# Gated feed-forwards, down product: five of eleven units as seven block products, at positions 1, 3, 5, 6 and 8, with the first set of weight sums made in the up steps

## What is computed

```
def _swiglu_ffn(x, g_norm, w_gate_up, w_down):      # FFN_HIDDEN = 2816, D_MODEL = 1024
    h = _rms_norm(x, g_norm)
    gate, up = jnp.split(h @ w_gate_up, 2, axis=-1)
    return (jax.nn.silu(gate) * up) @ w_down
```

## Time and profile before

| | us |
|---|---|
| median of 3 runs (lowest, highest) | 1206.88 (1206.46, 1207.20) |
| the profiled execution, device time | 1207.01 |
| its span, first to last instruction | 1205.3 |
| PE busy | 1197.1 (99% of the span) |
| PE weight loads busy | 1028.9 (85%) |
| DVE busy | 945.8 (78%) |
| ACT busy | 705.1 (59%) |
| POOL busy | 54.8 (5%) |
| HBM read | 218.31 MB |

### The profile page before, as it was taken

One profiled execution on the slowest core, in us unless ns is written; L12 is line 12 of the kernel. 1 busy time (PEld: TensorE's weight loads), 2 busy tenths in 40 slices (PEclk: granted clock), 3 DMA queues, 4 the chain that ended last, 5 costly groups with the idle time before them and its releaser, 6 DMA issues.

```text
span 1205.3 us, 17062 instructions
## 1 busy us (share of the span) xinstructions
PE 1197.1 (99%) x6787; PEld 1028.9 (85%) x6787; DVE 945.8 (78%) x1133; ACT 705.1 (59%) x821; POOL 54.8 (5%) x105
## 2 busy tenths in 40 slices
PE   9999999999999999999999999999999999999998
PEld 7888888888899888888888888988888888988886
DVE  5566476669786686767978995999987998699986
ACT  7655264555465665555638565577654765477752
POOL 2000000000010000000010020000001011000000
PEclk9999999999999999999999999999999999999999
DMA  9644636555654335655554444455564434556550
GB/s 347 239 157 165 237 140 215 193 185 179 238 191 170 132 140 209 210 177 189 188 205 167 148 144 170 174 211 189 196 216 169 146 105 175 180 187 209 195 192 35
DMA packets 32567, 220.36 MB, mean 183 GB/s; under 512 B 3889, under 2 KB 4049, under 8 KB 6769
## 3 DMA queue, kind: packets, MB, share of 16 engines
q1 hardware_dynamic: 29888, 212.33, 49.6%
q0 software_dynamic: 1664, 5.41, 1.3%
q10 hardware_dynamic: 944, 1.64, 0.4%
HBM read 218.31 MB, written 1.05 MB: 182 GB/s over the span
## 4 chain that ended last, share of the span: by engine, by line
PE 92%; DVE 6%; DMA 1%; issue 0%; POOL 0%; ACT 0%; ACTq 0%; POOLq 0%; DVEq 0%
PE acc L1969 16%; PE acc L1971 16%; PE acc L1970 16%; PE tb L2003 10%; PE acc L2003 9%; PE tb L2006 5%; PE acc L2006 5%; PE tb L2013 3%; DVE cacc L1645 3%; DVE wlo L1212 1%; PE acc L2333 1%; PE acc L2335 1%; PE acc L2336 1%; PE tb L1970 1%; PE tb L1971 1%; PE tb L1969 1%
## 5 line engine op out<-in xcount | busy, mean ns | idle before, releaser
L1212 DVE TENSOR_TENSOR wlo<-raw,whi 128x2048 fp32r<-128x2048 f32 x184 | 418.9, 2287 | 124.4 <-ACT whi L625 124.4
L625 ACT ACTIVATE whi<-raw 128x2048 fp32r<-128x2048 f32 (+1 forms) x198 | 370.3, 1883 | 115.4 <-PE acc L1971 69.5
L1969 PE MATMUL acc<-whi,xth 128*128 128x512 f32 x448 | 179.5, 401 | 0.4 <-DVE xtl L1310 0.3
L1971 PE MATMUL acc<-whi,xtl 128*128 128x512 f32 x448 | 174.9, 390 | 0.0
L1970 PE MATMUL acc<-wlo,xth 128*128 128x512 f32 x448 | 174.5, 390 | 0.0
L1969 PE MATMUL acc<-whi,yth 128*128 128x512 f32 (+1 forms) x428 | 168.7, 394 | 0.0
L1971 PE MATMUL acc<-whi,ytl 128*128 128x512 f32 (+1 forms) x428 | 166.5, 389 | 0.0
L1970 PE MATMUL acc<-wlo,yth 128*128 128x512 f32 (+1 forms) x428 | 166.2, 388 | 0.0
L2003 PE MATMUL tb<-xhl,whi 128*128 128x512 f32 x512 | 121.9, 390 | 0.0
L2003 PE MATMUL acc<-xhl,whi 128*128 128x512 f32 x480 | 114.2, 390 | 0.0
L2003 PEld LDWEIGHTS tb<-xhl,whi 128*128 128x128 f32 x512 | 94.9, 188 | 19.4 <-issue 0.5
(11 more groups left out here) (422 smaller groups left out, 1752.2 us busy)
## 6 DMA issues: line engine op xcount, KB each, us to landing
raw<-in_stream SPq DMA_DIRECT2D x200, 1024.0 KB, 4.9
rb<-in_rel_rows POOLq DMA_DIRECT2D x8, 256.0 KB, 2.9
x<-in_x_in ACTq DMA_DIRECT2D x4, 256.0 KB, 7.3
raw<-in_stream SPq DMA_DIRECT2D x2, 512.0 KB, 9.2
gs_sb<-in_gs_row POOLq DMA_DIRECT2D x1, 1024.0 KB, 7.8
frow<-in_fin_row POOLq DMA_DIRECT2D x2, 512.0 KB, 4.7
raw<-in_stream SPq DMA_DIRECT2D x2, 256.0 KB, 6.9
ws_sb<-in_ws_t POOLq DMA_DIRECT2D x1, 512.0 KB, 7.5
```

The lines of the kernel that those rows point to most:

```text
L625: act.activation(whi[:, s, c0:UNIT], raw[:, s, c0:UNIT], ACT.Copy).then_inc(hi_ready, 1)
L1212: dve.tensor_tensor(wlo[:, s, :], raw[:, s, :], whi[:, s, :], ALU.subtract).then_inc(lo_ready, 1)
L1969: pe.matmul(o, xh, wh, start=first, stop=False)
L1971: return pe.matmul(o, xl, wh, start=False, stop=last)
```

## The change

`SEVEN` goes from 4 to 5 and `SEVEN_POS` from (2, 4, 6, 7) to (1, 3, 5, 6, 8), for both gated feed-forwards. The order of hidden steps changes with it. The first set of weight sums (position 1) is made in up loop 7 from a second copy of its unit, `tcopy`, which POOL loads after the third up step. The second set (position 3) is made by DVE right after the up loops. The order of DVE's and ACT's work in the down stage is written anew. The last seven runs p1, p6, p5, p7, p2, p4, p3, with the wait for its weight sums right after p1. The fold comes after `lo` of the next stage's first unit and before that of the second. The load of `frow` waits for the last seven's `tb` products rather than for position 7. The sums of y have buffers of their own for each seven, the fifth one in the place of `us`.

```diff
-SEVEN = 4
-SEVEN_POS = (2, 4, 6, 7)
-DOWN_ORDER = (0, 1, 3, 2, 5, 4, 7, 9, 6, 8, 10)
+SEVEN = 5
+SEVEN_POS = (1, 3, 5, 6, 8)
+DOWN_ORDER = (0, 3, 1, 5, 2, 6, 7, 4, 9, 8, 10)
+STAGED = (0,)
+STAGE_STEP = (7,)
...
+        wsum_at = (o_xh, o_sc + 5120)
+        tcopy = at("tcopy", [2048], o_xh + 2048)
...
+            def stage(e, U0):
+
+                pool.wait_ge(unit_used, U0 + 6)
+                pool.dma_start(tcopy[:, :], stream[down_at(e) + SEVEN_POS[0]]).then_inc(t_copied, 16)
+
...
             rms_diagonals(1)
+            stage(0, U_GLU0)
             root(2)
...
             rms_diagonals(3)
-            pool.wait_ge(unit_used, U_DOWN1 + SEVEN_POS[-1] + 1)
+            stage(1, U_GLU1)
+            pool.wait_ge(y_banks, 8 + 2)
...
# ScalarE, glu
                     low_kept(j - 1)
                     hi(U0 + 2 * j + 3)
                     silu_sum(j - 1)
+                    if j == CTF:
+                        y_sums_hi(4, CTF - 2)
+                        y_high(CTF - 1)
+                        sums_hi(e, 1)
                     hi(U0 + 2 * j + 4)
-                    y_high(j - 1)
-                for j in range(1, CTF):
-                    if j == CTF - 2:
+                    if j < CTF:
+                        y_high(j - 1)
+                    if j in STAGE_STEP:
+                        sums_hi(e, STAGED[STAGE_STEP.index(j)])
+                for j in range(5, CTF + 2):
+                    if j == CTF + 1:
                         first_sum(e)
-                    if j >= 3:
-                        hi(U0 + 2 * CTF + j + 2)
-                    if j in (1, 3, 5, 6):
-                        sums_hi(e, (1, 3, 5, 6).index(j))
+                    hi(U0 + 2 * CTF + j)
+                    if j in (5, 6, 8):
+                        sums_hi(e, {5: 2, 6: 3, 8: 4}[j])
...
# VectorE, sums and glu
-                if i >= 1:
+                if staged:
+                    dve.wait_ge(t_copied, 128 + 16 * (e + 1))
+                elif i >= 1:
                     dve.wait_ge(unit_used, down_at(e) + (SEVEN_POS[i - 2] + 1 if i >= 2 else 0))
...
                     if place in SEVEN_POS:
                         y_sums(j - 1, SEVEN_POS.index(place))
-                    if U0 + 2 * j + 4 <= down_at(e) + SEVEN_POS[1]:
+                    if j in STAGE_STEP:
+                        sums(e, STAGED[STAGE_STEP.index(j)])
+                    if j < CTF:
                         lo(U0 + 2 * j + 4)
-                    if U0 + 2 * j + 4 == down_at(e) + SEVEN_POS[0]:
-                        sums(e, 0)
                     y_low(j - 1)
-                    if place in SEVEN_POS:
+                    if place in SEVEN_POS and j < CTF - 1:
                         y_sums_lo(SEVEN_POS.index(place))
-                for j in range(1, CTF):
-                    if j >= 3:
-                        lo(U0 + 2 * CTF + j + 2)
-                    if j in (1, 3, 5, 6):
-                        sums_lo(e, (1, 3, 5, 6).index(j))
-                    if j + 2 in SEVEN_POS:
-                        sums(e, SEVEN_POS.index(j + 2))
-                    if j == CTF - 3:
+                    if j in STAGE_STEP:
+                        sums_lo(e, STAGED[STAGE_STEP.index(j)])
+                y_sums_lo(4)
+                sums(e, 1)
+                for j in range(4, CTF + 2):
+                    if j == CTF + 1:
                         fold_sums(e)
+                    lo(U0 + 2 * CTF + j)
+                    if j in (4, 5, 6, 8):
+                        i = {4: 1, 5: 2, 6: 3, 8: 4}[j]
+                        if i > 1:
+                            sums(e, i)
+                        sums_lo(e, i)
...
# TensorE, seven
                 p1()
-                if e >= 2 and last:
-                    pe.wait_ge(side_lo, y_lo_count(e, len(sevens(e)) + i + 1))
+                def t_ready():
+                    pe.wait_ge(side_lo, t_lo_count(e, "t", i) if e < 2 else y_lo_count(e, 2 + i + 1))
+
+                if last:
+                    t_ready()
                     p6()
                     p5()
                     p7().then_inc(y_banks, 1)
...
                 p3()
-                pe.wait_ge(side_lo, y_lo_count(e, len(sevens(e)) + i + 1))
+                t_ready()
                 p5()
                 p7()
-                mm = p6()
-                if last:
-                    mm.then_inc(y_banks, 1)
+                p6()
                 p4().then_inc(unit_used, 1)
```

More of the change, by code:

```diff
@@ L168, in two_blocks_kernel @@
         xhl = at("xhl", [KT, 2 * SEQ], o_sc + 5120, F32R)
[L170 to L173, removed]
+        main_at = [(o_sc + 2048 + 3 * P * i, o_sc + 2048 + 3 * P * (4 + i)) for i in range(4)]
+        main = [(at(f"ysum{i}", [3 * P], a), at(f"ysum_h{i}", [3 * P], b, F32R), at(f"ysum_l{i}", [3 * P], a, F32R))
+                for i, (a, b) in enumerate(main_at)]
+        late = [(at(f"ysum_late{i}", [3 * P], a), at(f"ysum_late_h{i}", [3 * P], b, F32R),
+                 at(f"ysum_late_l{i}", [3 * P], a, F32R))
+                for i, (a, b) in enumerate(((o_sc + 1024, o_sc + 1536), (o_sc + 1536, o_sc + 1024), (o_sc + 512, o_sc)))]
+        wsum_at = (o_xh, o_sc + 5120)
+        tcopy = at("tcopy", [2048], o_xh + 2048)
         wsum = [at(f"wsum{i}", [2048], o) for i, o in enumerate(wsum_at)]
@@ L406, in y_hi_count, with t_hi_count, t_lo_count, t_made_before @@
         def y_hi_count(e, n):
-            return 3 + 9 * min(e, 2) + 5 * max(e - 2, 0) + n
+            return 3 + 11 * min(e, 2) + 5 * max(e - 2, 0) + n
         def w_hi_count(e, n):
-            return y_hi_count(e, (SEVEN if e < 2 else 2) + n)
+            return y_hi_count(e, 2 + n)
         def y_lo_count(e, n):
-            return 3 + 8 * min(e, 2) + 4 * max(e - 2, 0) + n
+            return 3 + 10 * min(e, 2) + 4 * max(e - 2, 0) + n
         def made_count(e, n):
-            return 2 + 36 * min(e, 2) + 22 * max(e - 2, 0) + n
+            return 2 + 44 * min(e, 2) + 22 * max(e - 2, 0) + n
+        def t_hi_count(e, what, i):
+            return y_hi_count(e, T_ORDER.index((what, i)) + 1)
+        def t_lo_count(e, what, i):
+            return y_lo_count(e, T_ORDER.index((what, i)) + 1)
+        def t_made_before(e, what, i):
+            before = T_ORDER[:T_ORDER.index((what, i))]
+            return made_count(e, sum(3 if w == "t" and n not in STAGED else 4 for w, n in before))
+        def y_sum(e, i):
+            return main[i] if i < 4 else late[e]
+        def is_staged(U):
+            return U in [down_at(e) + SEVEN_POS[i] for e in range(2) for i in STAGED]
         def is_seven(U):
@@ L627, in sums_hi @@
             def sums_hi(e, i):
-                f, h, _ = w_sums(e, i)
-                act.wait_ge(lo_ready, down_at(e) + sevens(e)[i] + 1)
+                f, h, _ = w_sums(e, 0 if e < 2 and i in STAGED else i)
+                if e < 2 and i in STAGED:
+                    act.wait_ge(side_made, t_made_before(e, "t", i) + 4)
+                else:
+                    act.wait_ge(lo_ready, down_at(e) + sevens(e)[i] + 1)
                 act.activation(h[:, :], f[:, :], ACT.Copy).then_inc(side_hi, 1)
@@ L798, in y_high, with y_sums_hi @@
                                    ACT.Copy).then_inc(g_hi, 1)
-                    if seven:
-                        c = slice(3 * P * i, 3 * P * i + 3 * P)
-                        act.activation(ysum_h[:, c], ysum[:, c], ACT.Copy).then_inc(side_hi, 1)
+                    if seven and j <= CTF - 3:
+                        y_sums_hi(i)
+                def y_sums_hi(i, j=None):
+                    if j is not None:
+                        act.wait_ge(g_lo, CTF * e + j + 1)
+                    act.activation(y_sum(e, i)[1][:, :], y_sum(e, i)[0][:, :], ACT.Copy).then_inc(side_hi, 1)
                 hi(U0 + 2)
@@ L1216, in sums @@
                 U = down_at(e) + sevens(e)[i]
-                s, n = U % SLOTS, made_count(e, 4 * len(sevens(e)) + 3 * i)
-                b12, b11, b22, b21 = (raw[:, s, 512 * b:512 * b + 512] for b in range(4))
-                t1, t3, t2, t4 = (w_sums(e, i)[0][:, 512 * b:512 * b + 512] for b in range(4))
-                if i >= 1:
+                s, n = U % SLOTS, t_made_before(e, "t", i) if e < 2 else made_count(e, 8 + 3 * i)
+                staged = e < 2 and i in STAGED
+                b12, b11, b22, b21 = ((tcopy[:, 512 * b:512 * b + 512] if staged else raw[:, s, 512 * b:512 * b + 512])
+                                      for b in range(4))
+                f = wsum[0] if staged else w_sums(e, i)[0]
+                t1, t3, t2, t4 = (f[:, 512 * b:512 * b + 512] for b in range(4))
+                if staged:
+                    dve.wait_ge(t_copied, 128 + 16 * (e + 1))
+                elif i >= 1:
                     dve.wait_ge(unit_used, down_at(e) + (SEVEN_POS[i - 2] + 1 if i >= 2 else 0))
@@ L1226, in sums @@
                 dve.wait_ge(side_made, n + 3)
-                dve.tensor_tensor(t4, b21, t2, ALU.subtract).then_inc(lo_ready, 1)
```

(15 more changed lines are left out.)

31 lines of the change are left out of this document (19 added, 12 removed).

## The result

| | before | after |
|---|---|---|
| median, us (6 runs each, same chip) | 1206.67 | 1217.30 |
| lowest, highest | 1206.24, 1207.20 | 1216.93, 1217.94 |
| span of the profiled execution | 1205.3 | 1215.5 |

The ratio is 1.0088, 95% interval 1.0078 to 1.0098. The forecast was 1217.7 us.

A forecast was written before the change was run, and what follows sets the result against it. TensorE's own pace was taken as the bound. Each stage was to lose 4.12 + 1.94 - 0.68 = 5.38 us; 2 x 5.4 = 10.8 on 1206.88 gave 1217.7 us, range 1213.0 to 1220.5.

The forecast's parts named there:

- The chain: Down stage: DVE's work from the last up step to the first `add`, ending at 59.66; transposes at 59.79, 5.39 later.
- The four gaps: Down stage: DVE idles for ACT at position 3 (3.88 us) and positions 5, 6, 8 (2.07 each), 10.1 us altogether.
- TensorE's own waits: Down stage: PE waits for weight sums at positions 3, 6 and 8, 4.12 us late in all; none at position 5.
- the restart of the transposes: Stage's end: transposes start 0.13 us after DVE's first `add` ends.
- The gain: Down stages: one more seven in each of two saves six matmuls, 1.36 us, 0.11% of the time.
- What was put at nothing: Up steps: added DVE and ACT work and the second unit load on POOL cost 0; so does the `frow` load.
- the bound of 249.0: Up loop after the staged sums: latest start of DVE's bank read if no other idle time absorbed the 6.2 us.
- the nearest row: Profile row used to price the added 1 MB load on POOL's queue: it lands in 7.8 us.
- DVE keeps up: Rival: DVE's chain 4 us shorter by position 8 and back at the fold in time; 1205.5 us, chance 0.08.
- The end absorbs the lateness: Rival: PE loses 4.1 us a stage but `add(0)` isn't late; 6.9 us in all, 1213.8 us, chance 0.08.
- The clock falls in the stalls: Rival: PE resumes at half clock, 2.0 us more at each stage's transposes; 1221.7 us, chance 0.08.
- A side remark that failed: Last seven: waiting after p1 cuts PE's lateness there (0.4, not 1.8), but the transposes' wait grows by the same.

The follow-up runs named there:

- e1_interleaved: Changed kernel with another unit's low part between a set's sums and their low part, and ACT's high part of position 4 ahead of the sums' copy: 1205.72 us.
- e6_interleaved_four: e1_interleaved with four sevens, at positions 1, 3, 5 and 6, and position 8 a normal unit of 24 matmuls: 1206.72 us.
- e2_act_order: Changed kernel with one swap on ACT, the high part of position 4 ahead of the copy of the second set of weight sums: 1209.69 us.
- e8_changed_filled: Changed kernel with five useless matmuls in each of its 1.6 us waits ahead of the transposes: 1217.79 us.
- e3_last_order: Changed kernel with the last seven in the order of the others, p1, p2, p3, then the wait for the sums' low part: 1220.09 us.
- e9_last_order_again: The same kernel as e3_last_order, run once more on another occasion: 1220.34 us.
- e4_longer_copy: Changed kernel with an extra 1024-wide ACT copy ahead of ACT's copy of each of the third, fourth and fifth sets of weight sums: 1223.27 us.

## Why the prediction was right, step by step

**The chain.** Times from the first down matmul (276.65 in the forecast's frame, 276.52 after):

| done | forecast | after |
|---|---|---|
| low part of the sums, position 3 | 17.72 | 17.65 |
| position 5 | 26.21 | 26.13 |
| position 6 | 34.70 | 34.60 |
| position 8 | 45.40 | 45.28 |
| first `add` | 59.66 | 59.49 |
| first transposes | 59.79 | 59.54 |

The four gaps were put at 3.88 and three of 2.07; the waits listed are 3.78 and three of 1.98, because a listed wait begins at the listed end of the instruction before, 0.08 behind the moment from which the forecast counts. From start to start (285.21 + 0.61 to 289.68) the first gap is 3.86. Every price came from start-to-start distances of instructions of the same shape in the trace of before, and that is why the sum of some thirty items is off by 0.2 us. The stage's length was read less well: the forecast said 62 to 63 us to the last product, from a stretch that ended 0.7 us short of it; it is 63.0.

**TensorE's own waits.** Position 6: 311.18 minus the start before it, 309.10, is 2.08, less the usual 0.23 it is 1.85 (forecast 1.93). Position 8: 321.86 - 319.95 - 0.23 = 1.68 (1.78). Position 3: no matmul wait is listed; its weight load alone stood for 0.29. What was mis-sized is the restart of the transposes: 336.06 follows the end of the `add` at 336.01 by 0.05, where I took 0.13 from a restart in the opening. Together with the chain's 0.17 that makes 5.14 rather than 5.39 per stage. Twice 5.14 is 10.3, where the forecast had 10.8. The 0.3 us outside the span wasn't in the forecast at all and has the other sign, so that the medians differ by 10.6. That the sum came within 0.4 us of the time is in part this luck.

**The gain.** 1.36 us for six matmuls: not visible in the changed kernel. In e1_interleaved against e6_interleaved_four it is 0.67 per stage in the traces and 1.0 in the medians.

**What was put at nothing.** The up steps keep their 111.00 us. DVE's bank read in the loop after the staged sums starts at 247.00, under the bound of 249.0. The second load of the unit lands in 5.3 us (median of the two), where the nearest row had 7.8. All three as forecast.

**The rivals.** *DVE keeps up* failed in the changed kernel and is what e1_interleaved is: its condition had two parts. A chain 4 us shorter was right for position 8: in e2_act_order, 3.8 us shorter, no wait for `wsum_l` is left. The other part, DVE back at the fold in time, needed more: there the transposes still wait 1.7 us. *The end absorbs the lateness* fell with the wait of 1.6 us at the transposes. *The clock falls in the stalls* didn't happen in the changed kernel, where both stages list 1.00 and e8_changed_filled gained nothing, but it was nearer than its chance of 0.08 says: waits of 2.5 to 3.0 us can bring it about, at 1.6 us each where the rival had 2.0.

**A side remark that failed.** The forecast said that it doesn't matter whether the last seven waits after p1 or after p3, since the transposes would make up for it. For DVE's chain that is so. For the time it isn't: one wait of 3.0 us in place of waits of 1.5 and 1.6 cost 2.8 us by the medians, by the clock. The order p1, p6, p5, p7 kept the changed kernel out of that.

Not tried: a sixth seven, and whether the staged copy is still needed once the order is mended.

## What to carry to other kernels

When work moves onto an engine that isn't the bound, write out that engine's instructions in their new order with start-to-start times, and look for a copy on another engine between two of them that depend on each other; a busy share (here 79%) says nothing of it. Put an independent instruction into each such gap before taking the idea for too expensive: the same work in another order was 11.6 us apart. A chain that is late shows up wherever the bounding engine happens to meet it, so cut it at its head, even where the visible wait is small.

## What the runs showed of the hardware

TensorE held its full clock behind waits of 1.5 to 1.7 us between dense stretches, in both stages of the changed kernel and at position 6 of e3_last_order. Behind waits of 3.0 us (e3_last_order, e9_last_order_again) it fell to its lower level in one of the two stages of each profile, and stayed in the upper one in the other, which goes with times scattered over 1.2 to 2.3 us. In e4_longer_copy it stayed behind a first wait of 2.9 us, fell behind the next, of 2.5 us, and fell behind one of 2.9 us in the second stage. So of seven waits of 2.5 to 3.0 us in three profiles four brought a fall; what decides between them isn't shown.

The slower starts begin at the restart itself or up to 1.3 us behind it. Those of e3_last_order and e9_last_order_again cost 1.6 us each (5.65 from the transposes to the next stage's first product, against 4.06). No profile caught an execution with two. The mean granted clock of each run points to them: it is 0.997 and 0.998 in the three runs of these two kernels that took 1218.9 to 1219.3 us, and 0.996 in the five that took 1220.2 to 1221.2 us, where 1217.3 + 2 x 1.6 = 1220.5 would be an estimate for two falls.

The Trainium skill, page "TensorE: Matmul & The Clock Gate", section "HAM oscillation — how this bites in real kernels", warns of idle gaps between bursts of matmuls. These traces agree for waits of 2.5 to 3.0 us, though not each time, and show none of it for 1.7. Useless matmuls in the gap, at 2.27 us a stage, bought 2.5 us.
